# Windowed attention in jobs of two heads whose products alternate between halves of the matmul array

## The reference, cut to what matters

```python
def dilated_group_attention(q, k, v, rel_bias, window, dilation):   # 16 heads of 64
    ...
    logits = jnp.einsum('bnqrhe,bnkrhe->bnrhqk', qs, kw,
                        preferred_element_type=jnp.float32) * scale + bias
    logits = jnp.where(valid[None, :, None, None], logits, NEG)
    lse = jax.nn.logsumexp(logits, axis=-1)
    p = jnp.exp(logits - lse[..., None])
    o = jnp.einsum('bnrhqk,bnkrhe->bnqrhe', p.astype(v.dtype), vw)
```

```python
    s = jnp.where(mask[None, :, None, None], s + bias, -jnp.inf)
    sink = sinks.astype(jnp.float32).reshape(Hk, G)[None, None, :, :, None, None]
    m = jnp.maximum(jnp.max(s, axis=-1, keepdims=True), sink)
    e = jnp.exp(s - m)
    a = e / (jnp.sum(e, axis=-1, keepdims=True) + jnp.exp(sink - m))
    o = jnp.einsum('bnhgqk,bnkhd->bnqhgd', a.astype(vb.dtype), vb).reshape(B, S, Hq * d)
```

## Time and profile before

| | |
|---|---|
| median of 3 runs | 4245.31 us (4244.09 to 4247.09) |
| the profiled execution | 4257.23 us, span 4255.4 us |
| mean granted TensorE clock | 0.922 of full |
| busy share | PE 90%, PEld 73%, DVE 40%, ACT 22%, POOL 44% |
| dilated stage, first scores to the start of the last job's values | 84.8 to 661.3 us |
| sliding stage, first scores to the next stage's first matmul | 2879.0 to 3049.0 us |

### The profile page before, as it was taken

How to read it: one execution, slowest core, us unless ns; L and a number is a source line. 1 busy time by engine, 2 the same in 40 slices (tenths; PEclk the granted TensorE clock), 3 DMA queues, 4 the chain that set the end, 5 groups by cost and what they waited for, 6 DMA issues and landing times. The chain is left out here.

```text
span 4255.4 us, 48445 instructions
## 1 busy us (share of the span) xinstructions
PE 3834.6 (90%) x18444; PEld 3108.9 (73%) x18444; DVE 1699.7 (40%) x2729; ACT 940.7 (22%) x2455; POOL 1891.3 (44%) x731
## 2 busy tenths in 40 slices
PE   8999996479788799999966899998899998979999
PEld 6877873368677588877855788875688877758887
DVE  2223336877626631132367411235331234642213
ACT  2333332111213410011033111015311112331111
POOL 5443430231243255555544456551156554335554
PEclk9999995788789899999977899998799999989999
DMA  3227850124222122222200222221122222222222
GB/s 133 88 90 99 97 88 12 44 75 95 70 86 70 54 100 99 95 93 84 99 20 1 82 99 91 99 85 50 60 84 95 99 89 91 70 75 90 91 97 79
DMA packets 95959, 342.08 MB, mean 80 GB/s; under 512 B 27078, under 2 KB 45766, under 8 KB 61208
## 3 DMA queue, kind: packets, MB, share of 16 engines
q1 hardware_dynamic: 83408, 314.22, 24.9%
q10 hardware_dynamic: 12360, 25.18, 1.7%
HBM read 318.39 MB, written 16.78 MB: 79 GB/s over the span
## 5 line engine op out<-in xcount | busy, mean ns | idle before, releaser
L294 POOL CAST wh<-raw 128x2048 fp32r<-128x2048 f32 x269 | 510.3, 1897 | 1883.4 <-PE bank L336 1498.6
L296 POOL TENSOR_TENSOR wl<-raw,wh 128x2048 fp32r<-128x2048 f32 x269 | 1242.6, 4619 | 21.5
L334 PE MATMUL bank<-XTh,wh 128*128 128x512 f32 (+1 forms) x2448 | 957.8, 391 | 44.9 <-DVE XTl L1028 15.1
L335 PE MATMUL bank<-XTh,wl 128*128 128x512 f32 (+1 forms) x2448 | 942.0, 385 | 0.0
L336 PE MATMUL bank<-XTl,wh 128*128 128x512 f32 (+1 forms) x2448 | 940.1, 384 | 0.0
L334 PEld LDWEIGHTS bank<-XTh,wh 128*128 128x128 f32 x2448 | 472.2, 193 | 159.6 <-issue 45.1
L336 PEld LDWEIGHTS bank<-XTl,wh 128*128 128x128 f32 x2448 | 470.8, 192 | 90.6
L335 PEld LDWEIGHTS bank<-XTh,wl 128*128 128x128 f32 x2448 | 471.8, 193 | 84.7
L334 PE MATMUL bank<-wh,XTh 128*128 128x512 f32 (+2 forms) x1056 | 392.5, 372 | 41.2 <-PEq L2059 15.2
L334 PE MATMUL bank<-wh,HTh 128*128 128x512 f32 x1024 | 404.8, 395 | 0.0
L335 PE MATMUL bank<-wh,HTl 128*128 128x512 f32 x1024 | 404.5, 395 | 0.0
(11 more groups left out here) (342 smaller groups left out, 4487.0 us busy)
## 6 DMA issues: line engine op xcount, KB each, us to landing
raw<-in_weights SPq DMA_DIRECT2D x270, 1024.0 KB, 4.8
B<-bias_d ACTq DMA_DIRECT2D x8, 1024.0 KB, 5.5
B<-bias_a ACTq DMA_DIRECT2D x8, 512.0 KB, 7.3
bias_d<-tab SPq DMA_DIRECT2D x16, 256.0 KB, 13.8
MO<-HS SPq DMA_DIRECT2D x64, 64.0 KB, 3.0
bc<-in_ln_g ACTq DMA_DIRECT2D x8, 512.0 KB, 6.6
bc<-in_ln_b ACTq DMA_DIRECT2D x8, 512.0 KB, 7.0
X<-in_x SPq DMA_DIRECT2D x4, 512.0 KB, 8.0
```

Of the source, the lines that this page charges most:

```text
L294: pool.tensor_copy(wh[s][:, :], raw[r][:, :]).then_inc(w_high.h, 1)
L296: pool.tensor_tensor(wl[s][:, :], raw[r][:, :], wh[s][:, :].bitcast(F32), ALU.subtract).then_inc(w_split.h, 1)
L334: nc.tensor.matmul(psum, sh, mh, start=first, stop=False)
L335: nc.tensor.matmul(psum, sl, mh, start=False, stop=False)
```

## The change

`RowAttention` now takes pairs of jobs, the same part of both heads. Scores of a pair are issued alternately for head 0 and head 1, each head into a bank of its own; so are the values, the two heads into the two halves of bank 6. SC, PT and the transposes have a place for each head (turn banks 4 and 5, or 4 and 1). The dilated stage has one pair of score banks (2, 3), so the scores of pair n wait for the bias adds of pair n-1; the sliding stage has two ((2, 3), (5, 7)). A turn is four pairs. `fill` is called at two places of a step, and a turn's tiles are made as two before the first transposes (after scores 0 and scores 1) and then two per step, around the scores of pair j+3; V is turned right behind tiles 1, 3 and 8. Copies out are of 128 partitions. VT and `tab` lie in the last slots of O3, whose order of axes changes; the last turn's first copy out waits until the tables are stored. The waits between small independent operations of VectorE are dropped, and the sum of the sink's exponential is moved from ScalarE to VectorE. The sliding stage is one stream of 16 pairs, all its biases loaded at its start, Q in four buffers; query tile 2 is made after scores 0, tiles 3 to 7 after the transposes of pairs 1, 3, 5, 7 and 9, and the splits of the output are done inside the stream.

```diff
-        DEPTH, SBANKS = 3, (2, 3, 5)
+        DEPTH = 3
+        PER_PAIR = (SC_DONE, SC_FREE, PV, OEV)
 
...
                 def scores(n):
                     ready(n)
-                    at(SC_FREE, max(n - DEPTH + 1, 0))
-                    for q, k, c, w in J[n].scores:
-                        r = nc.tensor.matmul(PS[SBANKS[n % DEPTH]][:, c:c + w], q, k, start=True, stop=True)
+                    at(SC_FREE, n - len(banks) + 1)
+                    for terms in zip(*(x.scores for x in J[n])):
+                        for e, (q, k, c, w) in enumerate(terms):
+                            r = nc.tensor.matmul(PS[banks[n % len(banks)][e]][:, c:c + w], q, k, start=True, stop=True)
                     r.then_inc(SC_DONE.h, 1)
 
                 def transposes(n):
...
+                    for e, x in enumerate(J[n]):
+                        at(PNORM, 2 * n + e + 1)
+                        at(PTC, 2 * n + e - 1)
+                        for k in range(x.ntiles):
+                            r = nc.tensor.transpose(PS[self.turn_banks[e]][:, P * k:P * k + P], SC[:, n % DEPTH, e, P * k:P * k + P], ident[:, :])
+                        r.then_inc(TR.h, 1)
 
                 def values(n):
                     placed(n)
-                    at(PTC, n + 1)
+                    at(PTC, 2 * n + 2)
                     at(OEV, n)
...
+                    for q, heads in enumerate(zip(*(x.values for x in J[n]))):
+                        last = len(heads[0]) - 1
+                        for m, terms in enumerate(zip(*heads)):
+                            for e, (v, tile) in enumerate(terms):
+                                r = nc.tensor.matmul(PS[6][64 * e:64 * e + 64, P * q:P * q + P], v, PT[:, e, P * tile:P * tile + P],
+                                                     start=(m == 0), stop=(m == last))
                     r.then_inc(PV.h, 1)
-                pe_jobs(len(J), DEPTH, scores, transposes, values, fill)
+                for d in range(DEPTH):
+                    scores(d)
+                    fill(-1, d)
+                for j in range(len(J)):
+                    transposes(j)
+                    fill(j, 0)
+                    if j + DEPTH < len(J):
+                        scores(j + DEPTH)
+                    fill(j, 1)
+                    values(j)
...
                 def normalise(n):
...
+                    for e, x in enumerate(J[n]):
+                        at(EXPED, 2 * n + e + 1)
+                        if self.sink is not None:
+                            link(v.tensor_tensor(self.stat(x, 2), self.stat(x, 2), self.stat(x, 0), ALU.add))
+                        link(v.reciprocal(self.stat(x, 3), self.stat(x, 2)))
...
                 def copy_probs(n):
-                    at(TR, n + 1)
-                    at(PV, n - 1)
-                    w = P * J[n].ntiles
-                    a.activation(PT[:, n % 2, 0:w], PS[4][:, 0:w], ACT.Copy).then_inc(PTC.h, 1)
+                    at(PV, n)
+                    for e, x in enumerate(J[n]):
+                        at(TR, 2 * n + e + 1)
+                        w = P * x.ntiles
+                        a.activation(PT[:, e, 0:w], PS[self.turn_banks[e]][:, 0:w], ACT.Copy).then_inc(PTC.h, 1)
...
+                for d in range(DEPTH):
+                    exps(d)
+                    drain(-1, d)
+                for j in range(len(J)):
+                    copy_probs(j)
+                    if j + DEPTH < len(J):
+                        exps(j + DEPTH)
+                    drain(j)
+                    copy_out(j)
...
+                    att = [RowAttention(jobs(h), SC, PT, stats, ((2, 3),), (4, 5)) for h in range(2)]
...
-                    V_TILE, V_STEP, QK_TILE = (0, 2, 7), (0, 2, 6), (4, 6, 9)
+                    V_TILE, V_STEP, QK_TILE = (0, 2, 7), (1, 3, 8), (4, 6, 9)
...
+                att = RowAttention(pairs, SC, PT, stats, ((2, 3), (5, 7)), (4, 1),
+                                   sink=lambda x: (sk[:, 0, x.head:x.head + 1], sk[:, 1, x.head:x.head + 1]))
+
+
+                def tile_at(j):
+                    if j == -1:
+                        return AHEAD_Q - 1
+                    return (j - 1) // 2 + AHEAD_Q if j % 2 and (j - 1) // 2 + AHEAD_Q < TILES else None
+
+                SPLIT_AT = {10: (0, 1), 11: (2, 3), 12: (4,), 13: (5,), 15: (6,)}
```

More of the change, by code:

```diff
@@ L1518, in biased @@
                         bias_done()
[L1519 to L1522, removed]
+                    for e, x in enumerate(J[n]):
+                        k = 0
+                        for c, m, w in x.rows:
+                            r = v.tensor_reduce(self.stat(x, 1)[:, k:k + m], bands(SC[:, n % DEPTH, e, :], c, m, w), AX.X, ALU.max, negate=True)
+                            k += m
+                        if self.sink is not None:
@@ L1544, in dve_links, with act @@
             def dve_links(self):
-                return sum(len(x.bias) - 1 + len(x.rows) - (self.sink is None) + 1 + len(x.rows) - 1 for x in self.jobs)
-            def act(self, at, copy_to, link=None, drain=lambda j: None):
-                a, J, SC, PT = nc.scalar, self.jobs, self.SC, self.PT
+                return sum(1 + 2 * (self.sink is not None) for n in self.pairs for x in n)
+            def act(self, at, copy_to, drain=lambda j, d=0: None):
+                a, J, SC, PT = nc.scalar, self.pairs, self.SC, self.PT
@@ L1618, in jobs @@
[L1618 to L1628 removed]
+                            by_group[0].append(window_jobs(e, (lambda b, q=qk(0): block(q, b)),
+                                                           (lambda b, n, k=qk(1): k[:, P * b:P * b + n * P]), vv(0), B[:, e, 0:W1]))
@@ L1691, in next_half, with place @@
                         return None if last and half == 1 else (half, 1 - half)
-                    def at_step(half, j):
-                        return [n for n, x in enumerate(tiles[half]) if x[4] == j]
+                    def place(j, d):
+                        return 2 * j + 2 + d if d < 2 else None
                     with nc.Block() as block:
@@ L1815, in _ @@
                             link.done()
[L1816 removed]
+                    for s in PER_PAIR:
+                        s.base += 32
+                    for s in (BIASED, EXPED, PNORM, TR, PTC):
                         s.base += 64
@@ L1917, in sliding_attention @@
                 PT = sb("PT", [P, 2, 512], F32, c)
                 stats = sb("stats", [P, 2, 4, 12], F32, c)
-                sinks = sb("sinks", [P, HEADS], F32, c)
-                sk = sb("sk", [P, 2, 4], F32, c)
-                js = []
-                for kv in range(2):
+                sk = sb("sk", [P, 2, HEADS], F32, c)
+                pairs = []
+                for n in range(TILES):
+                    kv = n % 2
+                    heads = []
                     for e in range(2):
```

334 lines of the change are left out of this document (149 added, 185 removed).

## The result

The changed kernel takes 4143.4 us (median of 4 runs, 4139.5 to 4150.9) against 4246.2 us: 102.8 us less, ratio 0.9765 with a 95% interval of 0.9747 to 0.9783. The forecast was 4166, 79 less.

What follows compares the result with a forecast made beforehand. TensorE was taken to bound the dilated stage, a chain over three engines the sliding one. Dilated -54.5 and sliding -24.6 total -79 off the 4245.3 us median: 4166 us, range 4132 to 4205.

Steps and rivals of the forecast that it cites:

- Scores overlap, 1.07 us with twice the records: Dilated stage's scores: the second head's products run free beside the first's, 7.1 to 4.1 us per turn, gain 3.0.
- Values, taken as free: Dilated stage's values: the second head costs no extra time, 7.7 to 3.9 us per turn, gain 3.8.
- the largest rival (0.20): Values products of the two heads don't overlap: only 44 us gained in all, 4201 us; chance 0.20.
- The slower rival: Every change of column side drains the array, 0.18 us at 352 changes, 63 us: 4260 us; chance 0.05.
- A turn of 69.6: Dilated stage, one pair of heads with the next pair's projections: 6.7 us less per turn, 69.6 us left.
- The new wait of 0.6 us before the second turn of V: Dilated turn: TensorE stands 0.6 us until ScalarE copies tile 2 out, after the exponentials of pair 3.
- The first normalisation, hidden by 2.3: Dilated turn: VectorE normalises pair 0 by 12.4 us, TensorE needs it at 14.7, so no wait.
- Seven turns, -47: Dilated stage's seven turns with projections, each 6.7 us shorter: 47 us gained.
- Last turn, -7.5: Dilated stage's eighth turn, without projections and set by VectorE's order: 34.5 to 27 us, gain 7.5.
- Sliding, -24.6: Sliding stage as one stream, from its scores to the next stage's matmuls: 169.9 to 145.3 us.
- my full-clock cycle: Sliding stage, two pairs and one projected tile: 15.2 us at full clock, TensorE idle about 4.1 us.
- low clock of 7 to 10 us in each cycle: Sliding stage: low clock in each cycle adds 2 to 5 us of matmul time; 18.5 us taken per cycle.

## Why the prediction was right, and where not

- **Scores overlap, 1.07 us with twice the records:** right (0.86 and 1.06 to 1.09). **Values, taken as free:** right, and this was the step with the largest rival (0.20). The rule that I weighed (the Trainium skill, TensorE: Matmul & The Clock Gate, "The mechanism"), that only a change of row group lets a weight load overlap, doesn't hold here: both heads use all 128 rows, and 16 records take 1.03 us.
- **The slower rival,** a drain at each change of column side, is excluded: alternating costs nothing, it gains 0.5 us per block (1.03 against 1.51).
- **A turn of 69.6:** 69.1. The new wait of 0.6 us before the second turn of V is there with 0.43, for the reason given (it goes when the copy moves ahead of the exponentials).
- **The first normalisation, hidden by 2.3:** the cover held, except for 0.6 us in the first turn, where GpSimd's splits hold the normalising products (2.67, 2.11 and 2.41 us there). I had counted each VectorE product at 0.7 us and never looked for long ones.
- **Seven turns, -47:** -41.2. The step that was off is the stall of 4.92 us at the jump back, which I kept in the forecast as it was. I took the gap as a constant of the kernel, though the trace of before has two jumps, 0.74 and 4.92. After the change they cost 2.91 and 11.02 us and low clock behind them; the turns by themselves gave 51. What is waited for are instructions; that the second pair of packets comes later because the table copies fill the denser turns fits, but isn't shown.
- **Last turn, -7.5:** -8.6 (in the trace with passes written out -5.4, so this one varies too).
- **Sliding, -24.6:** -40.7, at the end of my range for it. Start 19.2 us against 20.3, five cycles 83.1 against 92.5, end 26.9 against 32.5. The mechanism (copies behind exponentials, one idle piece per cycle) was right. From wait to wait the cycles take 19.4, 16.1, 18.0, 16.2 and 14.1 us, the first and third with a stall of the minimum, which I hadn't seen; the last, the only one at a clock of 1.00, is 1 us under the 15.2 of my full-clock cycle. The mis-sized term is the low clock of 7 to 10 us in each cycle: in the changed kernel's five cycles it follows only the long gaps. Four traces of the same code in this stage took 129.2, 129.2, 130.8 and, at a clock of 0.76, 140.0 us. The stage's time isn't one number; the forecast of 145.3 lies above all of them.
- **What I left out:** 13.5 us from tiles moved by 32 bytes. I had counted what the change spares in work, and not that a scratch tile of 32 bytes goes and moves what lies behind it. It and the warm sliding stage outweigh the gaps, which is why the time fell by 24 us more than forecast. That part of the gain is luck and no merit of the alternation: with the 32 bytes put back the kernel takes 4168.2 us, 78 to 80 less than before. That this is so near the forecast of 4166 is luck as well, of a sliding stage sized too long and jumps sized too short.
- The 11.9 us between the profiled execution of before and its median stood at 7.5 after; taking the sum off the median was right to within 4.4.

## What to carry to other kernels

Two streams of small products in different halves of the array, row halves or column halves, run together if they are issued alternately, and partly even if they aren't. When a stage gets denser, look again at its waits for instructions: here each jump back of TensorE's loop waited for two packets of them, and passes written out had no such gap. A stall that is removed in a stage with other gaps may come back as low clock, so compare the stage's granted clock and TensorE's idle time beside its time. And when a change moves tiles in memory, look at products that it doesn't touch.

## What the runs showed of the hardware

- The pace of 128x512 products depends on the address of the stationary tile: 226.7, 228.9 or 233.3 ns for one and the same program, by 32 or 64 bytes.
- VectorE's tensor-tensor instructions with both operands in SBUF, its tensor-scalar ones and its copies are held until GpSimd's running instruction ends (0.23 to 4.03 us, 0.69 to 4.89). Those that read PSUM, tensor-reduce and the reciprocal aren't: in the changed kernel's trace 33 tensor-reduce and 19 reciprocal instructions start inside a split and take no longer than elsewhere. The Trainium skill (GPSIMD Engine Reference, "Specifications") names the interface shared with VectorE, for two SBUF inputs or a two-port mode; the trace agrees, down to 2 elements per partition.
- TensorE started records of the other half ahead of three issued before them, in both blocks read.
- A jump back of TensorE's loop cost from 0.43 to 11.36 us, and ended each of the 22 times 1.59 to 1.86 us after the second of two 16 KB instruction packets had landed.
